# The depthwise convolution of an FFN, moved from TensorE's diagonal matmuls to ScalarE and VectorE, in a two-layer encoder trunk

## What is computed

```python
def dwconv3(x, w):          # centred depthwise conv over positions, width 3
    ...
def short_conv_mixer(xn, w_in, conv_w, w_out):
    b_g, c_g, h = jnp.split(xn @ w_in, 3, axis=-1)
    return (b_g * dwconv3(c_g * h, conv_w)) @ w_out
...
def conv_ffn(xn, w_up, conv_w, conv_b, w_down):
    g, u = jnp.split(xn @ w_up, 2, axis=-1)
    g = dwconv3(g, conv_w) + conv_b
    return (jax.nn.silu(g) * u) @ w_down
...
    for i in range(DEPTH):                       # DEPTH is 2
        h = rmsnorm(x, norm_w[i, 0])
        if i % N_MIXERS == 0:
            x = x + short_conv_mixer(h, ...)     # layer 0
        else:
            x = x + dilated_attention(h, ...)    # layer 1
        h = rmsnorm(x, norm_w[i, 1])
        x = x + conv_ffn(h, ffn_up[i], ffn_conv_w[i], ffn_conv_b[i], ffn_down[i])
    return rmsnorm(x, final_norm)
```

## Time and profile before

| | |
|---|---|
| runs of the kernel before | 4236.60 and 4687.69 us, median 4462.14 us |
| the profiled execution's own time | 4239.66 us |
| its span, slowest core (core 3 of 0 to 7) | 4236.3 us |
| spans of the eight cores | 4198.0 to 4236.3 us |
| TensorE busy | 3615.3 us, 85% |
| VectorE busy | 1439.2 us, 34% |
| ScalarE busy | 865.6 us, 20% |
| GpSimd busy | 68.1 us, 2% |

### The profile page before, as it was taken

How to read it: one execution, slowest core, us unless ns; L and a number is a source line. 1 busy time by engine, 2 the same in 40 slices (tenths; PEclk the granted TensorE clock), 3 DMA queues, 4 the chain that set the end, 5 groups by cost and what they waited for, 6 DMA issues and landing times.

```text
span 4236.3 us, 59319 instructions; the slowest of 8 cores (4198.0 to 4236.3 us)
## 1 busy us (share of the span) xinstructions
PE 3615.3 (85%) x21892; PEld 1984.3 (47%) x21892; DVE 1439.2 (34%) x2569; ACT 865.6 (20%) x1592; POOL 68.1 (2%) x27
## 2 busy tenths in 40 slices
PE   0699995997699869984999999994999899969996
PEld 0345542553355435542675767672454345434543
DVE  0233332442243324321353535353333334323321
ACT  0222211111111111100343343422111111111110
POOL 0000000100000000001000000000000000000000
PEclk9999997998799989997999999997999899979998
DMA  9995216999822552245100000004115611451134
GB/s 115 150 142 95 71 54 120 122 150 219 176 67 87 161 149 73 86 137 171 61 17 19 17 19 17 19 2 141 58 43 169 230 58 65 168 199 59 51 138 142
DMA packets 330967, 427.19 MB, mean 101 GB/s; under 512 B 57920, under 2 KB 316736, under 8 KB 320832
## 3 DMA queue, kind: packets, MB, share of 16 engines
q1 hardware_dynamic: 155296, 284.47, 21.7%
q0 software_dynamic: 123856, 55.05, 12.3%
q10 hardware_dynamic: 51536, 83.89, 7.3%
HBM read 398.75 MB, written 133.17 MB: 126 GB/s over the span
## 4 chain that ended last, share of the span: by engine, by line
PE 76%; DMA 14%; DVE 4%; ACT 3%; issue 1%; SPq 1%; ACTq 0%; DVEq 0%; POOLq 0%
PE bank L574 14%; PE bank L586 14%; PE bank L638 10%; PE bank L737 7%; PE bank L394 7%; PE bank L596 5%; DMA F_wd<-wb_dn 4%; PE bank L765 4%; PE bank L440 3%; PE bank L304 2%; PE bank L826 2%; DMA wb_ci<-conv_in 2%; PE bank L828 2%; ACT F_sq L296 2%; PE bank L804 2%; PE bank L806 2%
## 5 line engine op out<-in xcount | busy, mean ns | idle before, releaser
L638 PE MATMUL bank<-F_a,F_wd 128*128 128x455 bf16 (+1 forms) x3168 | 654.8, 371 | 109.2 <-DMA F_wd<-wb_dn 98.1
L574 PE MATMUL bank<-F_xn,F_w 128*128 128x456 bf16 (+1 forms) x3168 | 638.3, 359 | 4.8 <-DVE F_xn L319 2.9
L586 PE MATMUL bank<-F_xn,F_w 128*128 128x455 bf16 (+1 forms) x3168 | 634.5, 357 | 0.0
L638 PEld LDWEIGHTS bank<-F_a,F_wd 128*128 128x128 bf16 x3168 | 319.4, 101 | 446.3 <-issue 170.5
L605 DVE TENSOR_TENSOR F_a<-bank,F_s 128x455 bf16<-128x455 f32 (+1 forms) x396 | 250.8, 633 | 737.8 <-ACT F_s L601 692.8
L601 ACT ACTIVATE F_s<-bank,vecs_sb 128x455 bf16<-128x455 f32 (+1 forms) x396 | 237.8, 642 | 1151.2 <-PE bank L596 1149.9
L574 PEld LDWEIGHTS bank<-F_xn,F_w 128*128 128x128 bf16 x3168 | 311.8, 98 | 311.6 <-issue 16.1
L586 PEld LDWEIGHTS bank<-F_xn,F_w 128*128 128x128 bf16 x3168 | 310.7, 98 | 302.4 <-issue 2.0
L737 PE MATMUL bank<-C_hn,C_w 128*128 128x512 bf16 x1536 | 345.0, 387 | 68.5 <-DMA C_hn<-hn_d 42.3
L394 PE MATMUL bank<-A_xn,A_wci 128*128 128x457 bf16 (+1 forms) x1728 | 340.9, 358 | 6.5 <-DVE A_xn L319 6.5
L810 ACT ACTIVATE C_p<-bank 128x256 bf16<-128x256 f32 (+1 forms) x768 | 236.4, 361 | 398.6 <-PE bank L806 385.7
(11 more groups left out here) (77 smaller groups left out, 2415.2 us busy)
## 6 DMA issues: line engine op xcount, KB each, us to landing
F_wd<-wb_dn SPq DMA_DIRECT2D x72, 1408.0 KB, 11.2
F_w<-wb_up SPq DMA_DIRECT2D x66, 1024.0 KB, 5.3
F_x<-x_d SPq DMA_DIRECT2D x16, 1820.0 KB, 11.3
wb_up<-ffn_up POOLq DMA_DIRECT2D x4, 5632.0 KB, 76.2
x_d<-F_x ACTq DMA_DIRECT2D x9, 1820.0 KB, 21.4
A_x<-xT SPq DMA_DIRECT2D x8, 1828.0 KB, 13.1
F_xp<-x_d SPq DMA_DIRECT2D x8, 1824.0 KB, 11.6
x_d<-A_x ACTq DMA_DIRECT2D x8, 1820.0 KB, 10.5
```

Source lines behind the costliest of these rows:

```text
L574: i = e.matmul(bk[:, 0:n], lhsT=wt[:, c, q * 128:(q + 1) * 128], rhs=xn[:, c, a0:a0 + n], start=(c == 0), stop=(c == KC - 1))
L586: i = e.matmul(bk[:, 0:n], lhsT=wt[:, c, (2 + q) * 128:(3 + q) * 128], rhs=xn[:, c, 1 + m0:1 + m0 + n], start=(c == 0), stop=(c == KC - 1))
L638: i = e.matmul(bk[:, 0:n], lhsT=wd[:, c, q * 128:(q + 1) * 128], rhs=a[:, c, m0:m0 + n], start=(c == 0), stop=(c == FCH - 1))
```

## The change

In both FFNs the depthwise convolution no longer runs on TensorE. For each piece ScalarE copies F_g times the first tap into an fp32 tile F_t (L590 of the changed kernel), VectorE adds the second and the third tap's products in place with two scalar_tensor_tensor operations (L594), ScalarE takes the Silu of F_t (L599) and VectorE multiplies with u as before (L603). There are two F_t tiles, and three F_s where there were four. The diagonal matrices and their tiles are gone from the FFN; part A keeps its own. Second, in part A, the loads of conv_in are a function `wci_load`: the first two stand behind the first x load, and the other four behind the first tile's norm.

```diff
@@ part A
-                for gi in range(6):
+
+                def wci_load(gi):
                     S.op("sp", lambda e, gi=gi: e.dma_start(
                         out=wci_sb[:, :, gi * 512:(gi + 1) * 512],
...
                 pro_a(0)
+                wci_load(0)
+                wci_load(1)
                 pro_b(0)
+                for gi in range(2, 6):
+                    wci_load(gi)
@@ FFN, tiles
-                sr = Ring([sb(f"F{li}_s{i}", [128, PM], BF16, st) for i in range(4)])
-                dr = Ring([sb(f"F{li}_dg{i}", [128, 3, 128], BF16, st) for i in range(3)])
+                sr = Ring([sb(f"F{li}_s{i}", [128, PM], BF16, st) for i in range(3)])
+                t2r = Ring([sb(f"F{li}_t{i}", [128, PM], F32, st) for i in range(2)])
@@ FFN, up_proj
-                            dg, rdg = dr.next()
-
-                            def mk(e, dg=dg, f=f):
-                                for tap in range(3):
-                                    i = e.tensor_scalar(out=dg[:, tap, :], in0=ident_f[:, :], scalar1=vcol(fcw + tap * FCH + f),
-                                                        scalar2=None, op0=ALU.mult)
-                                return i
-                            S.op("dve", mk, reads=[r_identf, r_vecs], writes=[rdg])
...
                             for pi, (m0, n) in enumerate(mp):
-                                bk, rbk = next_bank()
-
-                                def cv(e, bk=bk, dg=dg, gt=gt, m0=m0, n=n):
-                                    for tap in range(3):
-                                        i = e.matmul(bk[:, 0:n], lhsT=dg[:, tap, :], rhs=gt[:, m0 + tap:m0 + tap + n],
-                                                     start=(tap == 0), stop=(tap == 2))
-                                    return i
-                                S.op("pe", cv, reads=[rdg, rgt], writes=[rbk])
+                                t2, rt2 = t2r.next()
+                                S.op("act", lambda e, t2=t2, gt=gt, m0=m0, n=n, f=f: e.activation(
+                                    out=t2[:, 0:n], in_=gt[:, m0:m0 + n], func=AF.Copy, scale=vcol(fcw + f)),
+                                    reads=[rgt, r_vecs], writes=[rt2])
+                                for tap in (1, 2):
+                                    S.op("dve", lambda e, t2=t2, gt=gt, m0=m0, n=n, f=f, tap=tap: e.scalar_tensor_tensor(
+                                        out=t2[:, 0:n], in0=gt[:, m0 + tap:m0 + tap + n], scalar=vcol(fcw + tap * FCH + f),
+                                        in1=t2[:, 0:n], op0=ALU.mult, op1=ALU.add),
+                                        reads=[rgt, r_vecs], writes=[rt2])
                                 stt, rstt = sr.next()
-                                S.op("act", lambda e, bk=bk, stt=stt, n=n, f=f: e.activation(
-                                    out=stt[:, 0:n], in_=bk[:, 0:n], func=AF.Silu, bias=vcol(fcb + f)),
-                                    reads=[r_vecs], writes=[rbk, rstt])
+                                S.op("act", lambda e, t2=t2, stt=stt, n=n, f=f: e.activation(
+                                    out=stt[:, 0:n], in_=t2[:, 0:n], func=AF.Silu, bias=vcol(fcb + f)),
+                                    reads=[r_vecs, rt2], writes=[rstt])
                                 ub, rub = ubanks[pi]
                                 S.op("dve", lambda e, ub=ub, stt=stt, f=f, m0=m0, n=n: e.tensor_tensor(
                                     out=a[:, f, m0:m0 + n], in0=ub[:, 0:n], in1=stt[:, 0:n], op=ALU.mult),
```

## The result

The changed kernel takes 1.028 times the time before, 95% interval 1.023 to 1.0329: slower, by about what was forecast (1.029). All ratios here leave out the executions in which one die ran longer at a lower clock, while the medians of all runs take them in. The median of all twelve runs is 4439.78 us (4339.02 to 4583.02), 10 us above the forecast range of 4275 to 4430; for the kernel before it is 4382.57 us over ten runs. The profiled execution took 4380.87 us, its slowest core 4379.2 us.

What follows compares the result with a forecast made beforehand. TensorE bounded the up projections before; after the change VectorE's order would, at 11.91 us a step. From 4239.66 us, +136 for the stages, +10 for half clock and -24 for the start gave 4362 us, range 4275 to 4430.

Steps and rivals of the forecast that it cites:

- the first term of the sum: Whole kernel: the profiled execution's own time before the change, 4239.66 us, to which the forecast's gains and losses were added.
- What leaves TensorE: Up projections: nine convolution matmuls a step go, 1.73 us each step, 228 us in all, leaving TensorE 9.26 us a step.
- The chain: Up projections: VectorE and ScalarE wait for each other in order, 11.91 us a step against 10.99 before.
- c: Up projections: ScalarE's scaled Copy of a piece into F_t, taken as 0.67 us.
- s1 and s2: Up projections: VectorE's two scalar_tensor_tensor additions for each piece, taken as 0.687 us each.
- The six stages: The six up-projection stages together: 1619.9 us against 1483.9, a loss of 136 us.
- The half clock behind each stage: Stage ends: TensorE idles for VectorE, then does some 3 us of work at half speed; +10 us over six stages.
- The start: Start: the early x load lets the second tile's norm sum start 27 us earlier; -24 us, between -10 and -35.
- TensorE stays the bound: Rival, up projections: the new work lies wholly beside the matmuls, time 3988 us; chance 0.06.
- Waits between VectorE's own operations cost nothing: Rival, up projections: additions start 0.60 us apart, step 11.07 us, time 4251 us, no change; chance 0.05.
- the reload of ScalarE's table: Rival, up projections: ScalarE reloads its table between Copy and Silu, adding 1014 us, time 5376 us; chance 0.03.
- shorter than summed: Rival, up projections: the chain binds but with a step below 11.62 us, so the loss is within 2%; chance 0.22.

Runs made afterwards that it cites:

- e2: Changed kernel with each product one piece later on VectorE, Copies one piece ahead on ScalarE, three F_t tiles; ratio 0.9398 to the kernel before.
- e3: Changed kernel without the third tap's addition, one scalar_tensor_tensor a piece in place of two; ratio 0.961 to the kernel before.
- e6: Changed kernel with each step ordered as three Copies, six additions, three Silus, three products, with three F_t tiles; ratio 0.9524 to the kernel before.
- e8: Changed kernel with all three Copies ahead of the first Silu on ScalarE, three F_t tiles, VectorE's order kept; ratio 1.0204 to the kernel before.
- e4: Changed kernel with six PSUM banks in the up projections in place of eight; ratio 1.0217 to the kernel before.
- e5: Changed kernel with F_t in bf16 in place of fp32; ratio 1.0238 to the kernel before.
- e1b: Kernel before with the new order of the start's loads alone, measured a second time, on another chip; ratio 0.9969 to the kernel before.

## Why the prediction came out as it did

**The range missed: the basis of the sum.** The step that failed is the first term of the sum. It starts from the time of one execution, 4239.66 us, and sets the median of the runs shown aside as "no execution's time"; neither the sum nor the range has a term for how far the median of all runs lies above that execution. By ten runs that median was 4382.57 us before, 143 above the basis, and 4439.78 now. Measured like with like, the account of the change itself holds: the ratio is 1.028 where 1.029 was forecast, and the two profiled executions differ by 4380.87 - 4239.66 = 141 us, where 122 were forecast. Between the two medians the difference is only 57 us; no run here shows why it is smaller, and a basis of 4382.57 with the same +122 would have been 65 us too high.

The slowest cores of the two profiled executions divide the 143 us between them (4379.2 - 4236.3) like this: -34 up to the first stage (690.9 against 725.2), +151 in the stages, and +26 in what lies outside of them (2053 against 2027).

**What leaves TensorE**: right. e2 runs a step in 9.25 us, forecast 9.26.

**The chain**: right, and the experiments show it as one. Forecast 11.91 us a step, measured 11.94. Taking out one link took out its price (e3), turning both engines' order dissolved it (e2, e6), turning ScalarE's alone did nothing (e8), and the rivals that the trace itself suggests, banks (e4) and the operation's pace by type (e5), changed nothing. Of the terms, c and Silu were 0.663 and 0.676 for 0.67, s1 and s2 0.689 for 0.687. Copy to addition was 0.10 (809.83 + 0.68 to 810.61), taken as 0.17; the last cast to the Copy was 0.15 (807.59 + 2.09 to 809.83), taken as 0.09, so the two errors nearly cancel, which is luck. The last addition to the Silu was 0.09, as taken.

**The six stages**: forecast +136 us, measured 1634.5 - 1483.9 = +151. The first cast came at 1150.25 - 1143.7 = 6.5 us and the table load stood in the chain, both as said. The average step, (1414.52 - 1162.87) / 21 = 11.98, is 0.07 above the sum's, which makes 9 of the 15 us. Most of the rest is in the two stages of the second FFN with the attention's projection, 274.0 and 272.7 us: TensorE does that work in its wait, but its last group waits for banks behind the last product.

**The half clock behind each stage**: the wait is there (16.02 us of idle, forecast 18 less 1.5, then 0.64 of full clock), but whether it costs +10 us is not shown. On die 0 the parts outside of the stages took 2001 to 2018 us, on die 1 2030 to 2053, and before 2008 to 2027 on all eight cores: by the medians die 0 lies 14 us below the kernel before, and die 1 22 above. From the end of the first stage to the start of the second, where the down projection waits for transfers, it took 161 to 180 us in place of 154 to 192. Transfers that have more time to land during a longer up stage may cover the cost on die 0; this was not tested, nor was what made die 1 longer.

**The start**: right. Forecast -24, measured -26 on the middle core at the first stage's beginning (715.0 to 689.4), and -24 at the end by e1b. The second x tile landed at 152.3, 5 us sooner than the forecast's 157.1: it was issued 3.5 us later but took 32.92 us in place of 41.3. The first conversion took 5.7 us longer. And the third tile's load no longer held TensorE at all: it ran L304 at 213.79 without a wait, where it had waited until 250.06.

**The rivals**: "TensorE stays the bound" had the size right, and e2 is that case: forecast 3988, the slowest core of e2's trace took 4007.9 us. It needed what the prediction named, something else for VectorE to do while the Silu runs. "Waits between VectorE's own operations cost nothing" is out: the second addition starts 1.48 - 0.69 = 0.79 us behind the first, not 0.60. So is the reload of ScalarE's table: the changed kernel's trace has 13 table loads on this core, as many as the kernel before. The chain was not shorter than summed either.

## What to carry to other kernels

Before work is moved to idle engines, write down one period of each engine's list in order, with every wait, and add up the loop that goes through them; a busy share of 43% over the span, or 64% inside the stages, doesn't show it. When two in-order engines hand a tile back and forth, put the consumer's last operation one tile later, behind the next tile's first ones: here that, with the Copies moved ahead and one more F_t tile, turned 1.028 into 0.94 (0.95 in the second measurement) with the same instructions. When TensorE is idle for a bank, look first at who frees the bank late: here two banks fewer left the step at 11.94 us. Last, before a sum is given a range, ask whether the time that it starts from is of the same kind as the one that it will be held against.

## What the runs showed that was not expected

A scalar_tensor_tensor of 455 or 456 columns takes 0.69 us from fp32 inputs, with one input in bf16 and all in bf16 (687, 689, 692 ns; the first is L319 of the earlier trace rows, with fp32 inputs). A wait of VectorE for its own last operation costs 0.19 us: from the start of a product to that of the next instruction it is 0.55 us where that one needs nothing of it, and 0.735 us where it has to wait for the result. And the gain of a shorter start, 24 us on the middle core, does not show in the time of the slowest core: ratios of 1.000 and 0.9969, with intervals of some 0.0055 to either side.
